# RWKV-7 mixing on one core: another order for VectorE inside a pair of heads

## The reference, cut to what matters

```python
kk = heads(k * k_k)
kk = kk / jnp.maximum(jnp.sqrt(jnp.sum(kk * kk, axis=-1, keepdims=True)), 1e-12)
...
k = k * (1.0 + (a - 1.0) * k_a)
o, S = _rwkv7_scan(r, decay, k, v, kk, a, S0)
mu = jnp.mean(o, axis=-1, keepdims=True)
var = jnp.mean(jnp.square(o - mu), axis=-1, keepdims=True)
o = (o - mu) * lax.rsqrt(var + RW_GN_EPS)
o = o * ln_w + ln_b
o = o + jnp.sum(r * k * r_k, axis=-1, keepdims=True) * v
return (o * g) @ w_o, S, h[:, -1]
```

## Time and profile before

| | us |
|---|---|
| median of 3 runs (range) | 3501.02 (3499.78 to 3502.53) |
| the profiled execution, its own time | 3500.84 |
| its span in the trace | 3499.2 |
| TensorE busy | 3332.0 (95% of the span) |
| VectorE busy | 1887.7 (54%) |
| the eight pairs (first mask of pair 0 to the end of pair 7) | about 1762 to 2217 |

### The profile page before, as it was taken

One profiled execution on the slowest core, in us unless ns is written; L12 is line 12 of the kernel. 1 busy time (PEld: TensorE's weight loads), 2 busy tenths in 40 slices (PEclk: granted clock), 3 DMA queues, 4 the chain that ended last, 5 costly groups with the idle time before them and its releaser, 6 DMA issues.

```text
span 3499.2 us, 77068 instructions
## 1 busy us (share of the span) xinstructions
PE 3332.0 (95%) x32788; PEld 3168.7 (91%) x32788; DVE 1887.7 (54%) x2957; ACT 1054.7 (30%) x1674; POOL 130.9 (4%) x247
## 2 busy tenths in 40 slices
PE   8999999998998999988989898899999999899997
PEld 7998899998777999988978777799999999799997
DVE  6667643445655543447457666553344666654343
ACT  3222322223554322223333333332223222232221
POOL 0000000001221000000000000000000000000000
PEclk9999999999999999999999899999999999999998
DMA  3222222223343222221200000122222222122221
GB/s 123 86 80 73 68 85 89 86 94 99 124 126 92 86 95 81 93 89 56 79 17 11 19 11 14 53 87 97 80 97 79 76 78 77 58 91 92 83 91 67
DMA packets 103584, 269.40 MB, mean 77 GB/s; under 512 B 12690, under 2 KB 45714, under 8 KB 103010
## 3 DMA queue, kind: packets, MB, share of 16 engines
q1 hardware_dynamic: 90338, 228.94, 20.1%
q0 software_dynamic: 13056, 37.64, 3.2%
HBM read 248.01 MB, written 18.52 MB: 76 GB/s over the span
## 4 chain that ended last, share of the span: by engine, by line
PE 79%; DVE 11%; DVEq 3%; ACT 3%; issue 2%; SPq 0%; DMA 0%; ACTq 0%
PE ps L559 63%; PE ps L985 4%; PE ps L660 3%; PE ps L977 1%; PE ps L691 1%; PE ps L707 1%; PE ps L1081 1%; DVE cell L2166 1%; DVE arena_r L1873 1%; DVEq L2429 1%; DVE arena L2033 1%; PE ps L685 1%; DVE rstd L1852 1%; DVEq L2165 0%; DVE h L2163 0%
## 5 line engine op out<-in xcount | busy, mean ns | idle before, releaser
L559 PE MATMUL ps<-arena_r 128*128 128x272 f32 x11136 | 1500.5, 293 | 67.4 <-DVE arena_r L2297 21.2
L559 PEld LDWEIGHTS ps<-arena_r 128*128 128x128 f32 x11136 | 1434.4, 191 | 109.0 <-issue 60.7
L559 PE MATMUL ps<-hb_r,arena_r 128*128 128x272 f32 x8448 | 1060.7, 288 | 0.4 <-DVE hb_r L1866 0.4
L559 PEld LDWEIGHTS ps<-hb_r,arena_r 128*128 128x128 f32 x8448 | 1058.5, 188 | 1.1 <-DVE hb_r L1866 0.8
L1368 ACT ACTIVATE arena_r<-ring 128x1024 fp32r<-128x1024 f32 (+1 forms) x240 | 275.3, 1147 | 913.0 <-PE ps L559 913.0
L1892 DVE TENSOR_TENSOR arena_r<-ring,arena_r 128x1024 fp32r<-128x1024 f32 (+1 forms) x240 | 319.6, 1332 | 142.9 <-ACT arena_r L1368 142.9
L1932 DVE TENSOR_TENSOR arena<-ps,rstd 128x544 f32<-128x544 f32 x88 | 63.7, 724 | 292.9 <-PE ps L559 292.9
L1953 DVE TENSOR_TENSOR x<-x,ps 128x544 f32<-128x544 f32 x64 | 46.2, 721 | 293.5 <-PE ps L559 293.5
L1350 ACT ACTIVATE arena_r<-ring 128x1024 fp32r<-128x1024 f32 x80 | 84.6, 1057 | 229.7 <-PE ps L559 224.8
L660 PE MATMUL ps<-arena 128*128 128x128 f32 x1024 | 140.0, 281 | 9.2 <-DVE arena L1996 6.8
L660 PEld LDWEIGHTS ps<-arena 128*128 128x128 f32 x1024 | 128.8, 195 | 13.1 <-issue 7.3
(11 more groups left out here) (387 smaller groups left out, 3099.6 us busy)
## 6 DMA issues: line engine op xcount, KB each, us to landing
ring<-in_w_up SPq DMA_DIRECT2D x176, 512.0 KB, 3.5
ring<-in_w_mix SPq DMA_DIRECT2D x112, 512.0 KB, 3.5
ring<-in_w_down SPq DMA_DIRECT2D x64, 704.0 KB, 4.0
arena<-in_hg_s POOLq DMA_DIRECT2D x16, 512.0 KB, 3.7
out_hg_so<-arena POOLq DMA_DIRECT2D x16, 512.0 KB, 2.9
ring<-in_w_hgout SPq DMA_DIRECT2D x16, 512.0 KB, 3.5
arena<-in_cache_k SPq DMA_DIRECT2D x128, 64.0 KB, 1.9
arena<-in_cache_v POOLq DMA_DIRECT2D x128, 64.0 KB, 2.2
```

What stands on the lines that cost most here:

```text
L559: mm = pe.matmul(PS[:, 2 * a + hf, 0:HALF], part[:, ws], rhs[:, o:o + HALF], start=start and n == 0, stop=stop and n == 2)
```

## The change

All of it is in VectorE's list. (1) `key_norm(n)` goes from behind `next_mask(3)` to in front of it, directly behind `update(2)`. (2) `spread(rw_vx[s], ...)` goes from behind `masked(n, "zkt")` to in front of the bonus, directly behind the subtraction of line 2488. (3) `normed(g)` is cut in two. Its first part ends with one `scalar_tensor_tensor`, (o * weight) * reciprocal, in place of two instructions. The second, `gated(g)`, is one `scalar_tensor_tensor`, (o + bias) + bonus, in place of the bias and the addition, and the multiplication by the gate. In pairs that have a next one, `gated` is not run for pair g, but for g-1 behind `update(3)`, that is one pair later. The last two `gated` run in pair 7 and behind it.

```diff
                     dve.reciprocal(rw_sq, rw_sq)
                     dve.drain()
-                    dve.tensor_tensor(o, o, rw_sq, ALU.mult)
-                    dve.drain()
-                    dve.tensor_scalar(o, o, gain(V_LNW, g), gain(V_LNB, g), ALU.mult, ALU.add)
-                    dve.drain()
-                    dve.tensor_tensor(o, o, of_pair(rw_K, g), ALU.add)
+                    dve.scalar_tensor_tensor(o, o, gain(V_LNW, g), rw_sq, ALU.mult, ALU.mult)
+
+                def gated(g):
+                    o = of_pair(rw_R, g)
+                    dve.drain()
+                    dve.scalar_tensor_tensor(o, o, gain(V_LNB, g), of_pair(rw_K, g), ALU.add, ALU.add)
                     dve.drain()
                     dve.wait_ge(S("rw_gn_ev"), upto(GN_EV, "g", g))
                     dve.tensor_tensor(o, o, of_pair(rw_V, g), ALU.mult).then_inc(S("rw_yb"), 1)
...
                     update(2)
+                    if more:
+                        key_norm(n)
                     next_mask(3)
-                    if more:
-                        key_norm(n)
                     update(3)
+
+                    if g >= 1:
+                        gated(g - 1)
                     sample_second_level(h)
...
                     dve.tensor_tensor(r, r, PS[:, 6, :], ALU.subtract).then_inc(S("rw_rd"), 1)
+                    spread(rw_vx[s], rw_tms[s][:, 0:HD])
                     if more:
                         bonus(n, 1)
...
                         masked(n, "zkt", rw_zkt[n % 2], 2, "strict")
-                    spread(rw_vx[s], rw_tms[s][:, 0:HD])
+                    elif former:
+                        gated(g)
...
                 normed(last)
+                gated(last)
```

More of the change, by code:

```diff
@@ L2464, in pair @@
                     update(2)
-                    next_mask(3)
                     if more:
                         key_norm(n)
+                    next_mask(3)
                     update(3)
+                    if g >= 1:
+                        gated(g - 1)
                     sample_second_level(h)
```

## The result

The changed kernel takes 3473.61 us (median of 6 runs, 3472.06 to 3477.66), the kernel before beside it 3500.85 us. The ratio is 0.9926 with a 95% interval of 0.9916 to 0.9936: 27 us faster by the medians, with 3473.0 forecast.

A forecast was written before the change was run, and what follows sets the result against it. TensorE, busy 95% of the span, bounds the kernel; in layer 2's pairs, a chain of waits between TensorE and VectorE. Terms 10.0 + 15.0 + 2.5 + 0.5 = 28.0 us off 3501.0 give 3473.0 us, range 3461 to 3489.

The forecast's parts named there:

- The wait in front of level 4: Middle of pairs 0 to 6: moving the key norm starts `level(4)` 1.43 us earlier in each, 10.0 us gained.
- 0.26 us to spare: Before `update(3)`: key norm and `next_mask(3)` end at 1892.21, ahead of TensorE's product at 1892.47.
- the signs by which the prediction called itself wrong: Clock still falling in the middle, `update(3)` held by VectorE's own list, or the tail's falls changing number or length.
- The clock in the middle: Between `level(4)` and `centred`: TensorE's fall to 1.2 GHz goes, 15.0 us gained, bounds 0 and 15.0; least certain term.
- My 5.95 us for the stretch: `level(4)` to `centred` at full clock: pair 7's 5.54 us, less 0.70 idle, plus 1.11 for the `rate` product.
- The rule that the prediction weighed against it: Middle: falls need a longer idle stretch, so the fall stays; 13.0 us gained, 3488.0 us; that rival's chance 0.16.
- `gated` in the middle: Behind `update(3)` in pairs 2 to 7: 1.6 to 1.7 us, hidden with under 0.1 us to spare; at most 10 us.
- The tail: End of pairs 1 to 6: `level_mask` starts 0.41 us earlier in each, 2.5 us gained.
- the cap: Tail: about 2.7 us leave VectorE's list but only 0.41 comes out, since `level_mask` then waits for TensorE's `matrix(n, 5)`.
- the 1.37 us left there: Tail: TensorE's idle time before the second `spread`, claimed to remain after the change.
- The end: Behind pair 7: the last group norm takes 2.40 us in place of 2.88, 0.5 us gained.

The follow-up runs named there:

- the kernels with memsets: The changed kernel with two or three delaying memsets, each behind a drain, ahead of the third update in pairs 0 to 6: 3487.31 and 3498.53 us.
- the run with the second spread first: The changed kernel with the second spread (of `rw_nx`) moved in front of the next pair's first level mask: 3450.69 us, ratio 0.9860.
- the same exchange: The kernel before, changed only by putting the second spread in front of the next pair's first level mask: 3488.32 us, ratio 0.9969.
- with the fifth update earlier as well: The changed kernel with the second spread before the next first level mask and `update(5)` ahead of the transition matrix's first product: 3446.02 us, ratio 0.9851.

## Why the prediction was right

**The wait in front of level 4 (10.0 us forecast).** The wait shrank from 1.69 to 0.29 us, 1.40 in each of 7 pairs, 9.8 us. VectorE's 0.44 us of idle time before the third update is what I had as 0.26 us to spare. But from `sample_state` to `level(4)` the six pairs gained only 7.0 us instead of 8.4. The stretch into pair 5 gave nothing: the fall behind pair 4's tail, short before (3.4 us), was long after (6.8 us). That is one of the signs by which the prediction called itself wrong (the tail's falls change their number or length): seven falls stayed seven, but one changed its length. I had taken the tail's clock as unchanged, and no run shows why this fall grew.

**The clock in the middle (15.0 us forecast).** It stayed at 2.4 GHz in all seven pairs. From `level(4)` to `centred` the sum over pairs 1 to 6 went from 49.1 to 35.3 us, 13.8 us; pair 0's stretch from `level(4)` to `sample_state` from 31.6 to 30.0. That is 15.3 us. My 5.95 us for the stretch, put together from pair 7, was 5.89. It was the term that could have failed, and the kernels with memsets, one run each, show its cause by themselves. The rule that the prediction weighed against it, from the Trainium skill's page "TensorE: Matmul & The Clock Gate", section "HAM oscillation — how this bites in real kernels", would have kept the falls and given 3488 us. These runs don't agree with it: waits of 1.2 to 1.9 us brought falls in 4 to 7 of 7 pairs, and a wait of 0.29 us in none.

**`gated` in the middle (0 forecast).** It cost nothing, as the run with it in the tail shows, though VectorE comes to `centred` in the same moment as TensorE's mean. The forecast of less than 0.1 us to spare was close.

**The tail (2.5 us forecast).** From the bonus to `sample_state` it went from 13.98 to 13.60 us, 0.38 in six pairs, 2.3 us. 2.7 us left VectorE's list and 2.46 us of idle time came up in their place: the cap was right. But I took the 1.37 us left there as given: the run with the second spread first shows that this wait, too, came from the order of VectorE's list and not from a late result. The spread in front of the bonus was free; 0.43 us of idle time is left there.

**The end (0.5 us forecast).** VectorE's last group norm took 2202.39 - 2200.03 = 2.36 us from its first `scalar_tensor_tensor` to the low parts, against 2.88. It was given back and more: the 84 products behind it ran 13.44 us where the kernel before took 12.32. After, the clock was low for 5.9 us of them (below, first the stretch of the changed kernel and its products), before for 3.4 us (then the same of the kernel before). This fall was not in my sum.

```profile
2203.20:2209.40 6.20, 6.20 (x28) 6.20 (x29) 4.22 (x6) 0.00 (x0) 0.00 (x0) 0.52 0.68 169
```

```profile
2203.16 13.44 PE L559 MATMUL ps<-arena_r 128*128 128x272 f32 x84 [1.93 <-DVE arena_r L2297]
```

```profile
2230.90:2235.20 4.30, 4.30 (x22) 4.30 (x23) 4.21 (x6) 0.00 (x0) 0.00 (x0) 0.60 0.70 148
```

```profile
2230.85 12.32 PE L559 MATMUL ps<-arena_r 128*128 128x272 f32 x84 [3.81 <-DVE arena_r L2297]
```

**The sum.** By terms the pairs and their end gained 25.0 us in the traces where 28.0 was forecast; the missing 3 us are the long fall into pair 5 (1.4), the end (1.1) and 0.35 us in pair 2, between two steps of the `rates`, which no wait in the trace explains. 1.6 us of the span's difference came ahead of the pairs and belong to no term. So the median is nearer to the forecast than the terms are, and that it came within 1 us is in part luck.

## What to carry to other kernels

Where an engine's instruction list is written by hand, look for a long instruction that stands in front of a step for which the bound engine waits, and move it to where that engine has work of its own. The 1.7 us wait was worth about twice its length in the middle of a pair (21 us in seven pairs with the key norm's move alone), because TensorE's clock fell behind it. Taking work off an engine is worth only the time until the next engine becomes the later one: 2.7 us taken out gave 0.4, while exchanging two steps of the same list, with nothing taken out, gave 23 us more. On the kernel before the same exchange gave 11 us, since VectorE came late to it there: what a step's place is worth depends on the rest of the list.

## What the runs showed of the hardware that was not expected

- A fall of the clock does not follow a wait strictly. In front of `level(4)`, behind the same products, it came in 0 of 7 pairs at 0.29 us (in each of five kernels), in 4 of 7 at 1.17, in 7, 7 and 5 of 7 at 1.69 and in 7 of 7 at 1.90.
- Falls in one place go with falls in another; which of them drives the other is not shown. Without the key norm's move, those in the middle were all long (8.9 to 9.0 us), those behind the tail short (3.4 us) in five of seven pairs, where the kernel before has one short and six long (6.8 us). The time of a stretch that was not changed can therefore move by 1.6 us either way.
- Falls come without a wait too. With the second spread first TensorE has no idle time in front of the state product, and the clock still fell for 3.4 us behind five of the seven tails (those of pairs 0, 1, 3, 5 and 6; with the fifth update earlier as well, 2 to 6).
- The exchange on the kernel before, in which falls went missing, scattered more than the kernel before beside it: 3477.7 to 3495.3 us in ten runs, against 3494.0 to 3503.3 us in thirteen.
